# First fetches of a routed expert stage taken from the token table itself, with the work around them reordered

## The chip, the cores and the metric

One core of one Trainium2 chip runs the whole kernel. The metric is the device time in microseconds. TensorE is PE in the profile (PEld is its weight load), VectorE is DVE, ScalarE is ACT, GpSimd is POOL, SyncE is SP (SPq and POOLq are the queues that issue DMAs).

## The reference

The kernel computes two transformer blocks of two layers each on 512 tokens of width 1024. In the first block each layer has a mixer (gated delta rule, then sparse attention), a layer norm, and a hierarchical mixture of experts. Only the mixture matters here:

```python
grp_p = softmax(xt @ w_grp + b_grp);  grp_prob, grp_idx = top_k(grp_p, 1)
e_logits = (xt @ w_rt + b_rt) of the chosen group          # 4 groups of 4 experts
top_p, top_i = top_k(softmax(e_logits), 2)                 # two experts per token
gate = grp_prob * top_p / sum(top_p)
for each of 16 experts:                                    # hidden width 256
    hdn = silu(xt @ wg) * (xt @ wu)
    acc += gate[:, expert] * (hdn @ wd)
```

Everything is float32.

## The kernel before, in words

**The stage.** `stage_experts` (L1815) runs once per layer. Every (token, expert) pair, 1024 in all, gets a slot; slots are grouped in blocks of 128 rows that share an expert. There are at least 16 blocks and at most 24 (`MAX_BLOCKS`); in the profiled execution both layers have 16. A block is: fetch its 128 token rows from memory (`h_rows`) with an indirect DMA, turn them on TensorE, multiply with the expert's gate and up weights, apply silu and the product, multiply with the down weights, and store 128 x 1024 results (`moe_rows`).

**Exact products from halves.** The gate and up product runs in the type fp32r. Weights `f` and inputs are split into a high part `h` (a copy, on ACT, `hi` L1789) and a low part `l` (the difference, `lo` L1793, 128x2048 elements), and three products hh, hl, lh are added. The gate and up weights of a block come as two units of 1 MiB (`load_in`, u = 0 and 1), the down weights as one of 1 MiB (`load_down`). There are two sets of buffers, b = 0 and 1, used by even and odd blocks. The down product takes `f` as plain f32.

**Routing.** Before the first block `Route` finds the slots. On VectorE: `slots` (L1652 to L1706) computes the two experts of each token and its slots; `rows` (L1709 to L1727) writes two sets of one-hot matrices, `named` (block of the slot, times the token's number, L1718 to L1723) and `in_row` (row inside the block, L1725; before the change it lies in the buffer `rt_y`). TensorE multiplies them, eight products of 128x128 by 128x24 in f32 (L1648), which gives the table row by block of token numbers. `tables` (L1738 to L1750) writes the experts of the blocks and the number of loop turns to `rt.table`, with instructions on one partition; SyncE, TensorE, ScalarE and GpSimd read it by register once `tabled` is counted. `tokens` (L1729 to L1736) reads the product, and writes the token numbers to `route.tok` as integers (L1736), which counts `indexed`.

**What GpSimd does.** It waits for `h_kept` (the token rows are in memory) and `indexed`. Its helper `fetch(i, b)` copies column i of `route.tok` into a tile `mine[b]` (L2024), waits for `picked`, adds two constants into the tile `passed` (L2026), and issues the indirect DMA with `mine[b]` as indices (L2027), which counts `x_loaded[b]`. It does so for blocks 0 and 1 at once, for later blocks when the rows of the block before have been turned. It also makes the low part of unit 1 for all blocks from the second on.

**What VectorE does.** Its order is: `slots`, `rows`, `tables`, `tokens`, the low parts of both units of block 0, then the low part of the turned rows, then per block: the low part of unit 0 of the next block, the product for `hid` (L2071), the low part of the next rows (L2062).

**What SyncE issues,** in program order: the constants `marks`, unit 0 of block 0 (L1781), the store of the token rows (L1868, 2 MiB), unit 1 of block 0, the down weights of block 0 (L1785), the loads for the stage after (L1872: in the first layer two of 512 KB and two of 4 KB, in the second only one of 4 KB). Then it waits for the first fetch (`x_loaded[0]`), and issues units 0 and 1 and the down weights of block 1. Later weights go out when their buffer is free: `turn_over` waits for `lo_ready` of each unit.

**The order of a block on TensorE:** gate and up products (24 products L1951, unit 0 then unit 1), turning of the next block's rows (L1930), down product of the block before (L1942), turning of `hid` (L1964). ScalarE's order in `body` is: `hidden` of the block before, `hi` of the next block's two units, silu (L2006), high part of the next rows (L1989), then `take`, the copy of the block before's result into `rt_y` (L1996), which waits until the store before it has landed.

```python
for b in range(2):
    fetch(BlockCount(b), b)                 # GpSimd, L2035
fetch_next(BlockCount(1), 1)
```

## Time and profile before

| | us |
|---|---|
| median of 3 runs | 2588.68 |
| the runs | 2580.58, 2588.68, 2588.92 |
| profiled execution, its own time | 2579.54 |
| its span | 2577.7 |
| PE busy in the span | 2332.3 (90%) |
| mean granted clock of PE | 0.948 of full speed |
| expert stage, first layer | about 545 to 751 of the span |
| expert stage, second layer | about 1166 to 1370 of the span |

A granted clock of 0.50 in a window is TensorE at 1.2 GHz, 1.00 is 2.4 GHz. Times below are from the start of the span. In a row of the timeline, "[a <-b]" at the end says that the engine was idle for a us before it and that b ended the idle time. Rows that follow each other are merged (x2, x8), with their whole stretch as duration.

### The profile page before, as it was taken

The page shows a single profiled execution, that of the slowest core. Times are in us where ns is not written, and L with a number is a line of the kernel's source. Part 1 is how long each engine was busy: PE and PEld are TensorE (multiplying, and loading weights), DVE is VectorE, ACT ScalarE, POOL GpSimd, SP SyncE. Part 2 cuts the span into 40 slices and gives each one's busy share as a digit, 9 for nine tenths or more (in the row PEclk, how much of TensorE's full clock was granted, in tenths as well). Part 3 has the DMA queues.
Part 4 walks back from the last instruction along what each step waited for, and adds up shares of the span by engine and source line. Part 5 has one row for each costly group of instructions (what it writes and reads, how often), then busy time and mean ns, then how long its engine had stood idle before and what let it go on. Part 6 is the DMA issues. An engine that isn't in the chain of part 4 may idle for free. (4 is left out here: it accounts for less than half of the span.)

```text
span 2577.7 us, 32698 instructions
## 1 busy us (share of the span) xinstructions
PE 2332.3 (90%) x12304; PEld 1810.2 (70%) x12304; DVE 1147.9 (45%) x2271; ACT 1047.9 (41%) x1830; POOL 853.7 (33%) x375
## 2 busy tenths in 40 slices
PE   6999999759969989995994899999997999999998
PEld 5888888656747866674763667678886767668886
DVE  3654642354436358754434453562223354462122
ACT  4443442216643247723664334533223334533222
POOL 2433532415552310023562222334332312224442
PEclk9999999769989999996997999999999999999999
DMA  6113110239983331017995311224222511315212
GB/s 138 49 50 115 42 50 30 90 137 393 401 296 84 135 105 44 30 51 261 396 406 191 102 49 62 90 67 147 97 66 76 172 33 50 119 50 164 98 66 74
DMA packets 190956, 327.15 MB, mean 127 GB/s; under 512 B 52544, under 2 KB 103056, under 8 KB 178528
## 3 DMA queue, kind: packets, MB, share of 16 engines
q1 hardware_dynamic: 183904, 300.08, 34.2%
q0 software_dynamic: 6912, 25.17, 2.6%
q8 instruction: 92, 1.51, 0.2%
q14 instruction: 48, 0.39, 0.0%
HBM read 293.62 MB, written 31.60 MB: 126 GB/s over the span
## 5 line engine op out<-in xcount | busy, mean ns | idle before, releaser
L159 POOL TENSOR_TENSOR branch_weights_wl<-branch_weights_wf,branch_weights_wh 128x2048 fp32r<-128x2048 f32 (+1 forms) x66 | 301.8, 4574 | 770.7 <-ACT branch_weights_wh L153 770.7
L153 ACT ACTIVATE branch_weights_wh<-branch_weights_wf 128x2048 fp32r<-128x2048 f32 (+1 forms) x66 | 124.6, 1889 | 200.2 <-PE merge_acc L207 92.9
L544 POOL TENSOR_TENSOR in_weights_wl<-in_weights_wf,in_weights_wh 128x1024 fp32r<-128x1024 f32 x32 | 79.5, 2486 | 237.1 <-ACT in_weights_wh L540 219.3
L207 PE MATMUL bmid_acc<-xh,branch_weights_wh 128*128 128x512 f32 x320 | 148.7, 465 | 9.1 <-PEq L72 9.1
L207 PE MATMUL merge_acc<-xh,branch_weights_wh 128*128 128x512 f32 x384 | 152.3, 397 | 3.4 <-PEq L72 3.4
L159 POOL TENSOR_TENSOR nsa_weights_wl<-nsa_weights_wf,nsa_weights_wh 128x2048 fp32r<-128x2048 f32 x13 | 59.5, 4585 | 282.2 <-ACT nsa_weights_wh L153 282.2
L207 PE MATMUL merge_acc<-xl,branch_weights_wh 128*128 128x512 f32 x384 | 152.1, 396 | 0.0
L207 PE MATMUL merge_acc<-xh,branch_weights_wl 128*128 128x512 f32 x384 | 152.0, 396 | 0.0
L207 PE MATMUL bmid_acc<-xh,branch_weights_wl 128*128 128x512 f32 x320 | 127.4, 398 | 0.0
L207 PE MATMUL bmid_acc<-xl,branch_weights_wh 128*128 128x512 f32 x320 | 127.3, 398 | 0.0
L1942 PE MATMUL exp_ps_y<-rt_wf,exp_ht 128*128 128x512 f32 x256 | 115.4, 594 | 2.9 <-ACT exp_ht L1984 1.9
L3274 ACT ACTIVATE bmid_pt<-bmid_x 128x256 f32<-128x256 f32 (+3 forms) x128 | 55.8, 436 | 141.6 <-PE bmid_x L3241 141.6
L568 PE MATMUL gmain_acc<-xh,in_weights_wh 128*128 128x512 f32 x256 | 110.6, 432 | 0.0
L1793 POOL TENSOR_TENSOR rt_wl<-rt_wf,rt_wh 128x2048 fp32r<-128x2048 f32 x16 | 76.9, 4804 | 79.8 <-ACT rt_wh L1789 79.8
L568 PE MATMUL gmain_acc<-xl,in_weights_wh 128*128 128x512 f32 x256 | 102.0, 398 | 0.0
L568 PE MATMUL gmain_acc<-xh,in_weights_wl 128*128 128x512 f32 x256 | 101.8, 398 | 0.0
L3611 ACT ACTIVATE merge_gate<-merge_acc,merge_gb 128x512 f32<-128x512 f32 x48 | 33.1, 689 | 148.8 <-DVE merge_merged L3639 75.2
L3637 DVE TENSOR_TENSOR merge_gate<-merge_gate,merge_b 128x512 f32<-128x512 f32 x32 | 22.0, 687 | 159.9 <-PE merge_b L3563 159.7
L207 PEld LDWEIGHTS merge_acc<-xh,branch_weights_wh 128*128 128x128 f32 x384 | 72.3, 188 | 21.3 <-issue 4.2
L1951 PE MATMUL exp_ps_gu<-rt_wh,xl 128*128 128x512 f32 x256 | 86.6, 410 | 0.4 <-DVE xl L2062 0.4
L207 PEld LDWEIGHTS merge_acc<-xh,branch_weights_wl 128*128 128x128 f32 x384 | 72.3, 188 | 17.3
L207 PEld LDWEIGHTS merge_acc<-xl,branch_weights_wh 128*128 128x128 f32 x384 | 72.4, 189 | 17.2
(659 smaller groups left out, 6209.0 us busy)
## 6 DMA issues: line engine op xcount, KB each, us to landing
branch_weights_wf<-w_in SPq DMA_DIRECT2D x56, 1024.0 KB, 5.1
rt_wf<-moe_w_out SPq DMA_DIRECT2D x32, 1024.0 KB, 10.2
rt_wf<-moe_w_in SPq DMA_DIRECT2D x32, 1024.0 KB, 9.2
in_weights_wf<-gdn_w_in SPq DMA_DIRECT2D x64, 256.0 KB, 3.4
nsa_weights_wf<-moe_w_in SPq DMA_DIRECT2D x16, 1024.0 KB, 9.9
moe_rows<-rt_y SPq DMA_DIRECT2D x64, 256.0 KB, 8.9
branch_weights_wf<-moe_w_in SPq DMA_DIRECT2D x16, 1024.0 KB, 9.8
merge_bwf<-w_branch SPq DMA_DIRECT2D x12, 1024.0 KB, 5.0
```

Of the source, the lines that this page charges most:

```text
L153: act.activation(self.h[u][:, :, 0:self.cols(b)], self.s.f[u][:, :, 0:self.cols(b)], ACT.Copy).then_inc(self.s.hi_ready, 1)
L159: pool.tensor_tensor(self.l[u][:, :, 0:self.cols(b)], self.s.f[u][:, :, 0:self.cols(b)], self.h[u][:, :, 0:self.cols(b)].bitcast(F32), ALU ...
L207: mm = pe.matmul(self.acc[:, s, 0:cols], lhs[:, P * s:P * s + P], rhs, start=(u == 0 and k == 0 and n == 0), stop=(u == 1 and k == HALF - ...
L544: pool.tensor_tensor(self.l[n % 3][:], self.f[n % 3][:], self.h[n % 3][:].bitcast(F32), ALU.subtract).then_inc(self.lo_ready, 1)
L568: mm = pe.matmul(self.acc[:, tile % 3, :], w[n % 3][:, k, P * s:P * s + P], x[:, HALF * u + k, :], start=(u == 0 and k == 0 and m == 0), s ...
L1793: eng.tensor_tensor(self.l[b][u][:], self.f[b][u][:], self.h[b][u][:].bitcast(F32), ALU.subtract).then_inc(self.lo_ready[u], 1)
L1942: mm = pe.matmul(ps_y[:, c, :], ht[:, k, :], w[:, k, c, :], start=(k == 0), stop=(k == 1))
L1951: mm = pe.matmul(ps_gu[:, 0, :].rearrange("p (c n) -> p c n", c=2), x[:, HALF * u + k, :], ws.by_matrix(w[b][u])[:, :, k, :], start=(u == ...
L3274: act.activation(self.pt[:, e, 0:width], self.ps_t[:, 0:width], ACT.Copy).then_inc(self.copied, 1)
L3611: act.activation(gate[:, f % 2, :], ws.acc[:, f, :], ACT.Sigmoid, bias=gb[:, n, 4 * j + f:4 * j + f + 1]).then_inc(ws.evicted, 1)
L3637: dve.tensor_tensor(gate[:, f % 2, :], gate[:, f % 2, :], ps_b[:, f, :], ALU.mult).then_inc(b_out, 1)
```

## The change

GpSimd's first two fetches use columns 0 and 1 of `route.tok` as indices directly (`fetch_first`): no copy to `mine`, no wait for `picked`, no addition into `passed`. The count that later fetches wait for on `picked` falls by two to match. VectorE's order becomes `slots`, `rows`, low part of unit 0 of block 0, `tokens`, `tables`, low part of unit 1. The one-hot matrices that TensorE multiplies are written as fp32r: `in_row` gets a tile of its own, and `named` times the token number goes to a new tile `named_r`. SyncE issues both gate and up units of block 1 before it waits for the first fetch; after the wait it issues the down weights of blocks 0 and 1, and then the loads for the stage after. All of it is in both layers.

```diff
--- before.py
+++ after.py
@@ -1621,8 +1621,9 @@
             ("step", "g_diff", "second", "exps"))
         self.onehot, self.counted, self.tabled = st.sem("r_onehot"), st.sem("r_counted"), st.sem("r_tabled")
         self.rowed, self.placed, self.indexed = st.sem("r_rowed"), st.sem("r_placed"), st.sem("r_indexed")
-        self.marks, self.in_row = marks, rt.y[:].rearrange("p (n r) -> p n r", r=P)
+        self.marks, self.in_row = marks, st.sb("in_row", [P, 2 * TT, P], F32R)
         self.reached, self.named = st.sb("reached", [P, 2 * TT, MAX_BLOCKS - 1]), st.sb("named", [P, 2 * TT, MAX_BLOCKS])
+        self.named_r = st.sb("named_r", [P, 2 * TT, MAX_BLOCKS], F32R)
         self.zero = st.sb("zero", [P, 1], I32)
         self.block, self.row = st.sb("block", [P, 2 * TT]), st.sb("row", [P, 2 * TT])
         self.spare, self.tok = st.sb("spare", [P, MAX_BLOCKS]), st.sb("tok", [P, MAX_BLOCKS], I32)
@@ -1645,7 +1646,7 @@
         for n in range(2 * TT):
             if n % TT == 0:
                 pe.wait_ge(self.rowed, n // TT + 1)
-            mm = pe.matmul(self.ps[:, 0, P:P + MAX_BLOCKS], self.in_row[:, n, :], self.named[:, n, :],
+            mm = pe.matmul(self.ps[:, 0, P:P + MAX_BLOCKS], self.in_row[:, n, :], self.named_r[:, n, :],
                            start=(n == 0), stop=(n == 2 * TT - 1))
         mm.then_inc(self.placed, 1)
 
@@ -1720,7 +1721,7 @@
         name = marks[:, P + n:P + n + TT]
         for k in range(2):
             named = self.named[:, TT * k:TT * k + TT, :]
-            link(dve.tensor_tensor(named, named, name.unsqueeze(2).to_broadcast([P, TT, MAX_BLOCKS]), ALU.mult))
+            link(dve.tensor_tensor(self.named_r[:, TT * k:TT * k + TT, :], named, name.unsqueeze(2).to_broadcast([P, TT, MAX_BLOCKS]), ALU.mult))
         for k in range(2):
             dve.tensor_tensor(self.in_row[:, TT * k:TT * k + TT, :],
                               self.row[:, TT * k:TT * k + TT].unsqueeze(2).to_broadcast([P, TT, P]),
@@ -1867,13 +1868,13 @@
                 ws.load_in(sp, 0, 0, 0)
                 sp.dma_start(g.h_rows.rearrange("(t p) d -> p t d", p=P), g.h[:]).then_inc(h_kept, 16)
                 ws.load_in(sp, 0, 1, 0)
-                ws.load_down(sp, 0, 0)
+                for u in range(2):
+                    ws.load_in(sp, 1, u, 1)
+                sp.wait_ge(x_loaded[0], 16)
+                for b in range(2):
+                    ws.load_down(sp, b, b)
                 for x, src in rt.loads:
                     sp.dma_start(x, src).then_inc(ln_in, 16)
-                sp.wait_ge(x_loaded[0], 16)
-                for u in range(2):
-                    ws.load_in(sp, 1, u, 1)
-                ws.load_down(sp, 1, 1)
 
                 def store(i):
                     for c in range(2):
@@ -2020,9 +2021,13 @@
 
             @block.gpsimd
             def _(pool):
+                def fetch_first(b):
+                    pool.indirect_dma_start(xr[b][:], None, g.h_rows[:, :],
+                                            bass.IndirectOffsetOnAxis(route.tok[:, b:b + 1], 0)).then_inc(x_loaded[b], 16)
+
                 def fetch(i, b):
                     pool.tensor_tensor(mine[b][:], route.tok[:, bass.ds(i(), 1)], route.zero[:], ALU.add).then_inc(picked, 1)
-                    pool.wait_ge(picked, i(1, 1))
+                    pool.wait_ge(picked, i(1, -1))
                     pool.tensor_tensor(passed[:], marks[:, 0:1], marks[:, 1:2], ALU.add)
                     pool.indirect_dma_start(xr[b][:], None, g.h_rows[:, :],
                                             bass.IndirectOffsetOnAxis(mine[b][:], 0)).then_inc(x_loaded[b], 16)
@@ -2033,7 +2038,7 @@
                 pool.wait_ge(h_kept, 16)
                 pool.wait_ge(route.indexed, 1)
                 for b in range(2):
-                    fetch(BlockCount(b), b)
+                    fetch_first(b)
                 fetch_next(BlockCount(1), 1)
                 pool.wait_ge(ws.lo_ready[1], 1)
                 ws.lo(pool, 1, 1, BlockCount(2))
@@ -2053,8 +2058,10 @@
                 dve.wait_ge(ld, 16)
                 route.slots(dve)
                 route.rows(dve)
+                ws.lo(dve, 0, 0, BlockCount(1))
+                route.tokens(dve)
                 route.tables(dve)
-                route.tokens(dve)
+                ws.lo(dve, 0, 1, BlockCount(1))
 
                 def x_lo(i):
                     for v in range(2):
@@ -2071,8 +2078,6 @@
                     dve.tensor_tensor(hid[:], act_g[:], ps_gu[:, 0, HID:512], ALU.mult).then_inc(hid_done, 1)
                     if not last:
                         x_lo(i.plus(1))
-                for u in range(2):
-                    ws.lo(dve, 0, u, BlockCount(1))
                 x_lo(BlockCount(0))
 
                 def scale():
```

## Rows read from the trace of the kernel before

**Rows 1.** Windows view, steady stretch: us, each engine's busy us (records), PEclk, DMA share, GB/s

```profile
640.00:660.00 20.00, 20.00 (x85) 13.99 (x84) 8.01 (x8) 13.10 (x16) 12.12 (x9) 1.00 1.02 416
```

**Rows 2.** Timeline, first layer, routing to first gate-up product: start, us, engine, line

```profile
559.72 1.29 DVE L1725 TENSOR_TENSOR rt_y<-exp_row,exp_marks 128x512 f32<-128x512 f32 x2
...
560.46 3.61 PE L1648 MATMUL exp_ps_t<-exp_named,rt_y 128*128 128x24 f32 x16 [5.86 <-DVE rt_y L1725]
...
564.11 0.24 DVE L1734 TENSOR_SCALAR exp_spare<-exp_ps_t,exp_marks 128x24 f32<-128x24 f32 x1 [1.45 <-PE exp_ps_t L1648]
...
564.69 4.49 DVE L1793 TENSOR_TENSOR nsa_weights_wl<-nsa_weights_wf,nsa_weights_wh 128x2048 fp32r<-128x2048 f32 x2
...
564.93 2.09 POOL L2024 TENSOR_TENSOR exp_mine<-exp_tok,exp_zero 128x1 int32<-128x1 int32 x1 [61.19 <-DVE exp_tok L1736]
...
569.40 1.12 POOL L2027 DMA_INDIRECT exp_xr<-h_rows,exp_mine  x1 [0.17 <-issue]
...
573.87 0.80 SPq L1781 DMA_DIRECT2D rt_wf<-moe_w_in  x2
...
576.52 0.77 PE L1951 MATMUL exp_ps_gu<-nsa_weights_wh,xl 128*128 128x512 f32 x1 [0.65 <-DVE xl L2062]
```

**Rows 3.** Windows view, the stretch while the fetch is being prepared

```profile
565.00:570.00 5.00, 0.00 (x0) 0.00 (x0) 4.18 (x2) 0.00 (x0) 4.75 (x3) 0.50 0.00 0
```

**Rows 4.** Timeline, first layer, between the first and the second block

```profile
584.79 1.03 PE L1930 MATMUL exp_ps_x<-ident,exp_xr 128*128 128x128 f32 x8
...
584.91 1.91 ACT L1789 ACTIVATE rt_wh<-rt_wf 128x2048 fp32r<-128x2048 f32 x1 [1.67 <-DMA rt_wf<-moe_w_in]
...
588.14 0.38 ACT L2006 ACTIVATE exp_act_g<-exp_ps_gu 128x256 f32<-128x256 f32 x1
...
589.88 0.76 PE L1951 MATMUL exp_ps_gu<-rt_wh,xl 128*128 128x512 f32 x1 [0.22 <-DVE xl L2062]
```

**Rows 5.** Timeline, first layer, second block's end and third block

```profile
596.76 1.03 PE L1930 MATMUL exp_ps_x<-ident,exp_xr 128*128 128x128 f32 x8
...
596.96 0.39 ACT L2006 ACTIVATE exp_act_g<-exp_ps_gu 128x256 f32<-128x256 f32 x1 [2.47 <-PE exp_ps_gu L1951]
...
601.21 0.48 PE L1951 MATMUL exp_ps_gu<-nsa_weights_wh,xl 128*128 128x512 f32 x1
...
606.80 1.03 PE L1930 MATMUL exp_ps_x<-ident,exp_xr 128*128 128x128 f32 x8
```

**Rows 6.** Timeline, second layer, end of first and of second block's gate-up products

```profile
1203.94 1.03 PE L1930 MATMUL exp_ps_x<-ident,exp_xr 128*128 128x128 f32 x8
...
1210.28 0.77 PE L1951 MATMUL exp_ps_gu<-rt_wh,xl 128*128 128x512 f32 x1 [0.16 <-DVE xl L2062]
...
1217.54 1.03 PE L1930 MATMUL exp_ps_x<-ident,exp_xr 128*128 128x128 f32 x8
```

**Rows 7.** Timeline, a fetch beside a low part on VectorE

```profile
592.05 2.35 DVE L1793 TENSOR_TENSOR nsa_weights_wl<-nsa_weights_wf,nsa_weights_wh 128x2048 fp32r<-128x2048 f32 x1 [1.72 <-ACT nsa_weights_wh L1789]
...
592.07 0.96 POOL L2027 DMA_INDIRECT exp_xr<-h_rows,exp_mine  x1
```

**Rows 8.** Timeline, the queue of SyncE, first layer

```profile
548.58 1.83 SPq L1872 DMA_DIRECT2D nsa_weights_ln_vectors<-ln_ffn_g  x1
...
552.89 1.21 SPq L1872 DMA_DIRECT2D nsa_weights_norm_shift<-by_feature  x1
...
574.72 0.59 SPq L1785 DMA_DIRECT2D rt_wf<-moe_w_out  x1
...
576.92 1.13 SPq L1781 DMA_DIRECT2D nsa_weights_wf<-moe_w_in  x2
```

**Rows 9.** Timeline, first layer, the last two of 16 blocks

```profile
714.00 1.31 ACT L1996 ACTIVATE rt_y<-exp_ps_y 128x512 f32<-128x512 f32 x2 [4.57 <-DMA moe_rows<-rt_y]
...
729.22 4.87 POOL L1793 TENSOR_TENSOR rt_wl<-rt_wf,rt_wh 128x2048 fp32r<-128x2048 f32 x1 [5.09 <-ACT rt_wh L1789]
...
732.32 0.48 PE L1951 MATMUL exp_ps_gu<-rt_wh,xl 128*128 128x512 f32 x1
```

## The prediction

> **What bounds the kernel now.** I first read the windows view over the first layer's expert stage. In its steady part TensorE is busy for all of every 20 us at full clock, and the DMA engines are busy all the time too, moving 416 GB/s [rows 1]. So two resources are at their limit together, and the question is which sets the pace. A block needs 4 MiB: 3 MiB of weights, half a MiB of fetched rows, half a MiB of stores. The third block's first gate-up product starts at 601.21 and the sixteenth's at 732.32 [rows 5, 9]: 13 blocks in 131.1 us, 10.09 each. TensorE's own work accounts for it: gate and up take 601.21 to 606.80, 5.59, and from there to the next block's first product 4.45 pass (596.76 to 601.21) [rows 5]; 5.59 + 4.45 = 10.04. From the third block on, TensorE sets the end, and what brings the third block forward brings the stage's end forward. The other demand, 4.19 MB in 10.09 us, is 416 GB/s: the transfers just keep up.
>
> Ahead of the third block the timeline shows TensorE waiting. The one-hot matrices are done at 561.01 (559.72 + 1.29), the table product starts at 560.46 and lasts 3.61, VectorE reads it from 564.11. GpSimd starts at 564.93, needs 2.09 for the copy of one column and as much for the addition, and issues the fetch at 569.40. SyncE sees the rows land at 573.87, and TensorE starts gate and up at 576.52 [rows 2]. While the fetch is prepared no byte moves [rows 3]. After the first block TensorE is late again: the second block's weights go out at 573.87, behind the fetch [rows 2]; ScalarE waits for their second unit, which it copies at 584.91, and only then does the first block's silu, at 588.14, though TensorE was through with gate and up at 584.79. The second block starts at 589.88 [rows 4].
>
> **The fetch, part by part.** Removed on GpSimd: the copy, the wait and the addition. From VectorE's start on the product (564.11) to GpSimd's first instruction 0.82 pass, and from there to the issue 4.47 [rows 2]. The 4.47 go, up to some 0.15 that a wait takes to end. The two are that long because VectorE's two low parts run just then (4.49 from 564.69, 2.24 each) [rows 2]. The Trainium skill (SBUF — State Buffer, Who interferes with whom) says that a VectorE instruction with two inputs in SBUF shuts out a GpSimd instruction that reads SBUF, for its whole length; by that rule the copy, which starts and ends with a low part, waited for the lock, and the trace agrees; the change removes it either way.
>
> Added ahead of `tokens` on VectorE: one low part, 2.24. It starts when the one-hot matrices are done, 561.05, and ends at 563.3. Beside it TensorE does the product. In f32 this is 8 products in 16 records over 3.61 [rows 2]; as fp32r I take one record each, half the time, 1.8: it ends by about 562.4, under the low part. (If the type saved nothing, it would end at 564.07 as now, and 0.8 of the gain below would go.) `tokens` starts at 563.3, the fetch goes out at 563.3 + 0.82 = 564.12 instead of 569.40: **5.28 earlier**. I keep the landing at 573.87 - 569.40 = 4.47 after the issue and the first gate-up product 2.65 after that (576.52 - 573.87) [rows 2]: 571.24.
>
> Moved behind `tokens`: `tables`, under 2 us of one-partition instructions, and the low part of unit 1, from about 565.8 to 568.1. Both lie under the flight of the fetch; the low part of the turned rows is not wanted before 570.4. SyncE needs the table only after the fetch has landed. Their cost is nothing as long as the fetch takes over 4 us; without that cover it would be 4. The new tile takes no time, and the writes as fp32r have the same elements; between nothing and 0.1 each I take nothing.
>
> **The weights.** Both units of block 1 now fill the idle stretch. In the first layer 6 MiB go ahead of the fetch before and after (the down weights and 1 MiB for the next stage change places with these two), so the queue is empty by 565 as in rows 3. In the second layer the next stage's loads are small: 1 MiB more goes ahead, 1.05 MB / 416 GB/s = 2.5 us [rows 1], about done when the fetch goes out. If the fetch and its neighbour share with it, the fetch lands up to 1.3 later (half a MiB); I take 0.
>
> With unit 1 in SBUF, ScalarE copies both units right after the turned rows, done by 575.1, and is free when gate and up end. The first block's gate-up took 584.79 - 576.52 = 8.27, part of it at the low clock (0.50 in the window before, rows 3). All at full clock it is 5.59, all at half 11.2: a gain of 2.7 or a loss of 2.9; I keep 8.27, since the same idle stretch stands before it. It ends at 579.51. In the undisturbed second block silu starts 0.20 after that point [rows 5], and the next block starts 1.74 after silu [rows 4]: 1.94 instead of 589.88 - 584.79 = 5.09. **3.15 gained**; should the table load ahead of silu not hide, 1.3 less. In the second layer the same gap is 1210.28 - 1203.94 = 6.34 [rows 6]: **4.40 gained**.
>
> The second block's gate-up took 596.76 - 589.88 = 6.88 [rows 4, 5], in the second layer 1217.54 - 1210.28 = 7.26 [rows 6]: after the idle wait the clock was low again. With TensorE idle for under 1 us at a time I take the full-clock 5.59: **1.29** and **1.67**; bounds are nothing and these.
>
> **What is late next.** The third block's weights. SyncE now has two down loads and, in the first layer, the next stage's loads (from 548.58 to 552.89 + 1.21 = 554.10, 5.5 of issuing [rows 8]) between the fetch and `turn_over`. Landing is seen at 568.6; 1.3 for the downs, 5.5, and the 1.6 that passed between 575.31 and 576.92 [rows 8] give 577.0: the very time of now. The queue holds 3 MiB and a fetch by then, gone by 577.3. The two units land near 582 and 584.5 (2.5 of transfer each, and an estimated 2 until it is seen); ScalarE is ready at 581.9. Its copies end at 586.4, GpSimd's low part (4.87 [rows 9]) at 591.3, and TensorE wants it at 591.6 + 2.8 = 594.4. That leaves 3.1 of margin. In the second layer the 5.5 are nearly absent. The down weights of block 0, moved past the fetch, land by 573 and are wanted at 588.
>
> **Sum.** First layer 5.28 + 3.15 + 1.29 = 9.72; second 5.28 + 4.40 + 1.67 = 11.35; together 21.1. One us off for margins that close late: at the last block GpSimd ends at 734.09 what TensorE wants at 732.32 + 2.8 = 735.1 [rows 9], 1.0 to spare in the first layer. **20 us.** The profiled execution took 2579.54 (span 2577.7 and 1.84 around it), which would give 2559.5. The median of the runs shown is 2588.68, 9.1 above; I set the gain against that: **2568.7**.
>
> **Rivals.** (1) The transfers set the pace, chance 0.2. ScalarE waits 4.57 for a store's landing late in the first layer [rows 9], so transfers have little left. Then the end moves only as the stream does: it restarts 5.28 earlier, and carries 1 MiB (2.5) less in the second layer: 13.1, plus the 1.0 that is spare. 14 us, 2574.7. Against it: TensorE's busy 20 of 20 [rows 1].
> (2) The fetch does not come earlier, chance 0.08: VectorE's low part of unit 1 or the weight loads hold it. For it, the copy of 2.09 in rows 2. Against it: a later fetch was issued in 0.96 beside a low part begun 0.02 before [rows 7]. The weights' part stays: 3.15 + 1.29 + 4.40 + 1.67 = 10.5, 2578.2. Were only the issue held, for one low part of 2.24 in each layer, 20 - 4.5 gives 15.5, 2573.2; rows 7 speak against it, `tables` stand between, and it has 0.03 of this 0.08. The Trainium skill's rule of SBUF — State Buffer, cited above, would do this if the fetch's reading of its indices counts as a read.
> (3) Little is left, chance 0.06: the early start is used up in both layers because the third block's weights are late by more than their 3.1 margin and the steady part starts no earlier than 4 us before now. Gain under 7.8.
> (4) Slower, chance 0.03. Place: ScalarE's wait for the store before it may write `rt_y` again; low parts of the next block queue behind. If TensorE starts earlier but stores land later, this loop can pass TensorE's 10.09. It costs 26 blocks times the excess; from 21.1 / 26 = 0.8 us per block on, all is lost, and at 1.1 the time is 7.5 above now, 2596.2. The 4.57 wait shows the loop is real [rows 9]; nothing in the change lengthens a store.
>
> **Chances and range.** What a measurement here can tell from no change is about 0.3%, 7.8 us. Forecast 0.63 and rivals (1) and (2) lie beyond it except for a part: faster 0.87, same 0.10, slower 0.03. The range takes in (1) and (2) at the upper end. At the lower end stands the full gain with the first blocks at the fast clock (21.1 + 5) from the median, 2562.6, or 20 from the lower level of the runs, 2560.6, with some room: 2556 to 2581.
>
> **What would show it.** The indirect DMA at about 564 and 1184.5, with no L2024 ahead of it; first gate-up product near 571.2; silu of the first block within 0.5 of gate-up's end; the second block's gate-up in 5.6; third block at 591.5 in the first layer; then 10.09 per block. Wrong: the third block early but the sixteenth not (rival 1), a fetch that lands more than 5.5 after its issue (2), ScalarE waiting for the third block's weights (3), a period above 10.4 (4).

## The result and the profile after

The changed kernel takes 2570.86 us (median of four runs, 2566.31 to 2572.63) against 2588.48 before (four runs, 2580.58 to 2588.92): a ratio of 0.9936, 95% interval 0.9913 to 0.9960. 2568.7 was forecast. The gain is 17.6 where 20 were expected, clear of no change and clear of the 0.3% that can be told here. Run again later, beside other kernels, it took 2568.10 against 2584.98, ratio 0.9938 (0.9921 to 0.9954).

The profiled execution took 2566.31, its span is 2564.5. The first rows are the timeline of the changed kernel, first layer, from the one-hot matrices to the first gate-up product, and answer to [rows 2]:

```profile
563.03 1.29 DVE L1726 TENSOR_TENSOR exp_in_row<-exp_row,exp_marks 128x512 fp32r<-128x512 f32 x2
563.78 1.88 PE L1649 MATMUL exp_ps_t<-exp_named_r,exp_in_row 128*128 128x24 f32 x8 [5.86 <-DVE exp_in_row L1726]
564.24 2.28 DVE L1794 TENSOR_TENSOR nsa_weights_wl<-nsa_weights_wf,nsa_weights_wh 128x2048 fp32r<-128x2048 f32 x1
...
566.45 0.23 DVE L1735 TENSOR_SCALAR exp_spare<-exp_ps_t,exp_marks 128x24 f32<-128x24 f32 x1
...
568.01 1.11 POOL L2025 DMA_INDIRECT exp_xr<-h_rows,exp_tok  x1 [62.21 <-DVE exp_tok L1737]
...
568.75 2.27 DVE L1794 TENSOR_TENSOR nsa_weights_wl<-nsa_weights_wf,nsa_weights_wh 128x2048 fp32r<-128x2048 f32 x1
569.42 2.42 POOL L2025 DMA_INDIRECT exp_xr<-h_rows,exp_tok  x1 [0.30 <-issue]
572.41 0.80 SPq L1786 DMA_DIRECT2D rt_wf<-moe_w_out  x2
...
575.05 0.76 PE L1952 MATMUL exp_ps_gu<-nsa_weights_wh,xl 128*128 128x512 f32 x1 [0.65 <-DVE xl L2069]
```

Absolute times do not compare, since this execution's stage began 3.31 later (548.61 against 545.30) with nothing changed ahead of it; in the twelve executions below it began anywhere from 544.26 to 548.07. So I count from the stage's first DMA issue in each layer, and write 19.40 for 568.01 - 548.61. The table product takes 8 records and 1.88 instead of 16 and 3.61, and hides under the low part. The fetch goes out at 19.40, before at 24.10. The *second* fetch's issue takes 2.42 where the first takes 1.11: a low part on VectorE began 0.67 before it.

Next, the timeline between first and second block, which answers to [rows 4] and [rows 5]. Silu now follows the end of gate and up (582.32) at once, the second block starts 2.10 after that end instead of 5.09, and its gate-up takes 5.67 instead of 6.88:

```profile
582.32 1.03 PE L1931 MATMUL exp_ps_x<-ident,exp_xr 128*128 128x128 f32 x8
582.51 0.39 ACT L2007 ACTIVATE exp_act_g<-exp_ps_gu 128x256 f32<-128x256 f32 x1 [2.58 <-PE exp_ps_gu L1952]
...
584.42 0.47 PE L1952 MATMUL exp_ps_gu<-rt_wh,xl 128*128 128x512 f32 x1 [0.57 <-DVE xl L2069]
...
590.09 1.04 PE L1931 MATMUL exp_ps_x<-ident,exp_xr 128*128 128x128 f32 x8
```

Then, still in the first layer, something that the forecast did not have. The timeline of the third block:

```profile
587.59 1.91 ACT L1790 ACTIVATE nsa_weights_wh<-nsa_weights_wf 128x2048 fp32r<-128x2048 f32 x1 [3.28 <-DMA nsa_weights_wf<-moe_w_in]
...
590.72 1.91 ACT L1790 ACTIVATE nsa_weights_wh<-nsa_weights_wf 128x2048 fp32r<-128x2048 f32 x1 [1.21 <-DMA nsa_weights_wf<-moe_w_in]
...
592.71 4.60 POOL L1794 TENSOR_TENSOR nsa_weights_wl<-nsa_weights_wf,nsa_weights_wh 128x2048 fp32r<-128x2048 f32 x1 [7.41 <-ACT nsa_weights_wh L1790]
...
594.82 2.51 DVE L1757 SCALAR_TENSOR_TENSOR exp_sg<-exp_e,exp_sg 128x4 f32<-128x4 f32 x1
...
597.77 6.98 DVE L2087 TENSOR_SCALAR h<-h 128x1024 f32<-128x1024 f32 x4
...
599.66 4.53 POOL L1794 TENSOR_TENSOR rt_wl<-rt_wf,rt_wh 128x2048 fp32r<-128x2048 f32 x1 [0.38 <-ACT rt_wh L1790]
...
604.67 2.28 DVE L1794 TENSOR_TENSOR rt_wl<-rt_wf,rt_wh 128x2048 fp32r<-128x2048 f32 x1
...
606.87 0.41 DVE L2078 TENSOR_TENSOR exp_hid<-exp_act_g,exp_ps_gu 128x256 f32<-128x256 f32 x1
...
607.34 0.44 PE L1965 MATMUL exp_ps_t<-ident,exp_hid 128*128 128x128 f32 x2 [2.56 <-DVE exp_hid L2078]
```

ScalarE waits for the third block's weights. GpSimd's low part of them runs to 597.31, and VectorE's instruction on 4 elements per partition, begun inside it, takes 2.51 and ends with it. The scaling of the rows (L2087, in the helper `scale`, once per stage) then takes 6.98. GpSimd's next low part begins inside it and ends at 604.19, and the scaling ends soon after. Behind it VectorE still has its own low part of the next block to make (604.67), and only then comes the `hid` product; TensorE waits 2.56. Which of VectorE's instructions is the one held is a matter of tenths: when this same kernel ran again (e11), the scaling got through and the low part behind it was held, with the same loss. Before, the same scaling fell between two low parts on GpSimd and took 2.50. This is the timeline of the kernel before:

```profile
594.57 4.57 POOL L1793 TENSOR_TENSOR nsa_weights_wl<-nsa_weights_wf,nsa_weights_wh 128x2048 fp32r<-128x2048 f32 x1 [1.54 <-ACT nsa_weights_wh L1789]
...
600.03 2.50 DVE L2082 TENSOR_SCALAR h<-h 128x1024 f32<-128x1024 f32 x4
...
606.34 4.83 POOL L1793 TENSOR_TENSOR rt_wl<-rt_wf,rt_wh 128x2048 fp32r<-128x2048 f32 x1 [5.50 <-ACT rt_wh L1789]
```

All kernels in one table. The positions are starts in the profiled execution, counted from the stage's first DMA issue, first / second layer. "hid 2" and "hid 16" are where TensorE turns (transposes) `hid` of the second and the sixteenth block (the loss just shown lies between hid 2 and hid 3, 12.9 where it should be 10.0; some expectations below call these the third and fourth block); the ratio is to the kernel before, run alongside.

| kernel | median us | ratio (95%) | fetch issued | hid 2 | hid 16 |
|---|---|---|---|---|---|
| before | 2588.48 | | 24.10 / 23.41 | 55.77 / 55.44 | 197.43 / 195.81 |
| changed | 2570.86 | 0.9936 (0.9913-0.9960) | 19.40 / 18.56 | 45.79 / 45.36 | 189.52 / 185.73 |
| e1 copies back | 2565.44 | 0.9927 (0.9904-0.9950) | 19.05 / 18.70 | 45.21 / 45.94 | 191.08 / 188.15 |
| e2 weights back | 2568.88 | 0.9944 (0.9930-0.9959) | 18.98 / 18.50 | 47.89 / 46.05 | 188.27 / 186.42 |
| e3 VectorE order back | 2576.83 | 0.9973 (0.9960-0.9986) | 18.43 / 17.98 | 47.72 / 45.88 | 195.24 / 186.25 |
| e4 f32 product | 2567.09, one run | | 20.11 / 19.61 | 47.44 / 45.64 | 187.81 / 185.98 |
| e5 scaling early | 2564.46 | 0.9913 (0.9892-0.9935) | 18.97 / 18.50 | 47.04 / 45.41 | 188.54 / 189.05 |
| e6 norm loads late | 2565.19 | 0.9921 (0.9898-0.9943) | 19.13 / 18.54 | 45.89 / 45.58 | 186.26 / 187.74 |
| e7 both (e5, e6) | 2567.18 | 0.9922 (0.9897-0.9946) | 19.40 / 18.50 | 47.04 / 45.05 | 187.41 / 185.41 |
| e8 VectorE order alone | 2571.12 | 0.9946 (0.9928-0.9963) | 20.37 / 19.62 | 48.36 / 48.26 | 188.70 / 193.60 |
| e9 two result buffers | 2566.59 | 0.9930 (0.9916-0.9945) | 19.34 / 18.56 | 45.73 / 45.43 | 188.96 / 185.72 |
| e10 e9 and e6 | 2561.84 | 0.9906 (0.9888-0.9924) | 19.01 / 18.59 | 45.32 / 45.44 | 185.61 / 185.73 |
| e11 changed again | 2568.10 | 0.9938 (0.9921-0.9954) | 18.97 / 19.64 | 45.76 / 45.92 | 189.33 / 186.29 |
| e12 e6 again | 2563.82 | 0.9920 (0.9904-0.9935) | 19.36 / 18.63 | 45.96 / 45.45 | 186.33 / 188.69 |

The gain of the two profiled executions splits like this. Up to hid 16 the first layer gained 197.43 - 189.52 = 7.91, the second 195.81 - 185.73 = 10.08, together 18.0. The rest of the kernel, unchanged, was 4.8 later (3.31 ahead of the first stage, 1.03 between the stages, 0.45 behind the second), which leaves the 13.2 that the spans differ by. The medians, over several runs, show 17.6, close to the stages' own 18.0. What lies outside the two stretches up to hid 16 took anywhere from 2184.4 to 2195.0 in the fourteen profiled executions, though no edit aims at it. That is more than most of the kernels below differ by, so a single execution's time says little, and the readings below go by positions inside the stage.

### The profile page after: what moved, and what is told of

Same layout as the page of the kernel before. It is cut to its first block and busy times, and to the rows that moved or that the text cites. A ratio compares the mean times of both kernels' runs of the same rounds, so it can differ in the third digit from the quotient of the medians.

```text
span 2564.5 us, 32648 instructions
## 1 busy us (share of the span) xinstructions
PE 2327.3 (91%) x12288; PEld 1804.1 (70%) x12288; DVE 1156.2 (45%) x2271; ACT 1046.7 (41%) x1830; POOL 850.1 (33%) x367
## 5 line engine op out<-in xcount | busy, mean ns | idle before, releaser
L727 ACT ACTIVATE gmain_x<-gmain_chunk 128x512 f32<-128x512 f32 x48 | 28.7, 597 | 137.1 <-PE gmain_chunk L658 137.1
```

The lines of the kernel that those rows point to most:

```text
L727: act.activation(self.x[i], self.B[i], ACT.Copy).then_inc(self.x_out[i], 1)
```

## The experiments

### e1: the copies back

```diff
-                    pool.wait_ge(picked, i(1, -1))
+                    pool.wait_ge(picked, i(1, 1))
...
                 for b in range(2):
-                    fetch_first(b)
+                    fetch(BlockCount(b), b)
```

> The changed kernel, but its first two fetches go through the copies again (copy, wait, addition, indirect DMA); all orders stay changed. Two readings of the two 2.1 us instructions before the change. Theory A (they were held by VectorE's low parts, and the new order of VectorE alone frees them): each takes 0.2, the first fetch is issued 18.9 to 19.6 after the stage's first DMA issue, where the changed kernel has 19.4 and 18.56 in its two layers, and the time is that of the changed kernel within 2 us, some 17 below before. Theory B (GpSimd's first instructions in a stage are slow by themselves, 2.1 each): the fetch goes out about 3.6 later in each layer and the time is about 7 us above the changed kernel.

Timeline of this kernel, first layer, GpSimd (the low part of unit 1 on VectorE begins at 564.95):

```profile
563.54 0.19 POOL L2029 TENSOR_TENSOR exp_mine<-exp_tok,exp_zero 128x1 int32<-128x1 int32 x1 [61.05 <-DVE exp_tok L1737]
563.81 0.19 POOL L2031 TENSOR_TENSOR exp_passed<-exp_marks 128x1 f32<-128x1 f32 x1
564.36 1.12 POOL L2032 DMA_INDIRECT exp_xr<-h_rows,exp_mine  x1 [0.36 <-issue]
565.51 1.76 POOL L2029 TENSOR_TENSOR exp_mine<-exp_tok,exp_zero 128x1 int32<-128x1 int32 x1
```

Theory A holds: 0.19 each instead of 2.09. The fourth row is the counterproof in the same trace: the copy for the second block, under a low part, takes 1.76. The fetch goes out at 19.05 and 18.70, no later than without the copies (19.40 and 18.56), since a direct fetch starts only 0.9 after the token numbers are written (566.93 + 0.18 to 568.01 in the changed kernel). Under the new order of VectorE the direct fetch, the part after which the change is named, is worth nothing that can be measured; the median is even lower than the changed kernel's, within the scatter. What it does under the old order shows in e3.

### e2: the weights back

```diff
-                for u in range(2):
-                    ws.load_in(sp, 1, u, 1)
-                sp.wait_ge(x_loaded[0], 16)
-                for b in range(2):
-                    ws.load_down(sp, b, b)
+                ws.load_down(sp, 0, 0)
                 for x, src in rt.loads:
                     sp.dma_start(x, src).then_inc(ln_in, 16)
+                sp.wait_ge(x_loaded[0], 16)
+                for u in range(2):
+                    ws.load_in(sp, 1, u, 1)
+                ws.load_down(sp, 1, 1)
```

> The changed kernel, but SyncE issues in the order of before: block 0's down weights and the next stage's loads first, both units of block 1 only after the first fetch has landed. Theory A (the pace is TensorE's, and the third block's start carries over to the end): the first fetch stays early, silu of the first block waits for ScalarE's copies again, the third block starts 4.4 later in the first layer and 5.5 to 6 later in the second than in the changed kernel, and the time is about 10 above it, 7.5 below before. Theory B (transfers set the pace): the same bytes go before the fetch in the first layer, so nothing is lost there, and 2.5 in the second.

Theory A had the direction and not the size. hid 2 comes 2.10 later in the first and 0.69 later in the second layer, not 4.4 and 5.5. ScalarE's copy of unit 1 starts 9.60 and 8.12 after SyncE's issue of the two units, where it started 11.04 and 11.15 after it before the change. The same loads land up to 3 sooner than before the change, because the DMA engines carry them faster (windows view under e3). At the end of the first layer this kernel is even ahead of the changed one (188.27 against 189.52): with its later second block the scaling misses GpSimd's low part. But the edit does two things. It also puts the next stage's loads back ahead of the fetch, out of the way of the third block's weights, which is what e6 does by other means. Beside e6 (186.26), which keeps the early weights, e2 is 2.0 late. So the early weights give 0.7 in the second layer and some 2 in the first, and in the changed kernel's first layer the place of the next stage's loads takes that back.

### e3: VectorE's order back

```diff
-                ws.lo(dve, 0, 0, BlockCount(1))
-                route.tokens(dve)
                 route.tables(dve)
-                ws.lo(dve, 0, 1, BlockCount(1))
+                route.tokens(dve)
+                for u in range(2):
+                    ws.lo(dve, 0, u, BlockCount(1))
```

> The changed kernel, but VectorE does tables, tokens, then both low parts, as before. GpSimd's first fetch is then ready to issue about 0.9 after tokens, inside the first low part. Theory A (a low part on VectorE that has begun holds an indirect DMA's issue on GpSimd until it ends): the issue record is 2 us or longer or begins after a low part's end, and the rows land 1.3 to 3.6 later than in the changed kernel; 2.5 to 7 us on the time. Theory B (the issue is not held, as one record of 0.96 beside a low part seemed to show): the fetch goes out 0.3 earlier than in the changed kernel and the time is the same or 1 us better.

Timeline, first layer, both engines:

```profile
561.70 4.49 DVE L1794 TENSOR_TENSOR nsa_weights_wl<-nsa_weights_wf,nsa_weights_wh 128x2048 fp32r<-128x2048 f32 x2
562.69 2.28 POOL L2025 DMA_INDIRECT exp_xr<-h_rows,exp_tok  x1 [59.78 <-DVE exp_tok L1737]
565.28 1.73 POOL L2025 DMA_INDIRECT exp_xr<-h_rows,exp_tok  x1 [0.30 <-issue]
```

The issue is held, 2.28 in both layers instead of 1.0 to 1.1. But it also starts 1.0 and 0.6 earlier, and the rows are seen at 24.05 and 23.71, only 0.25 and 0.85 later than in the changed kernel: theory A's mechanism, well under its price. Against the kernel before, the rows still land 4.5 and 4.1 sooner, with VectorE's order as it was: dropping the copies and the shorter product bring that. So the new order and the direct fetch stand in for each other, and either alone brings most of the early fetch (for the order alone see e8).

The time is 6 to 9 above the changed kernel's all the same. The profiled execution, the fastest of the ten, shows 5.7 of it behind the fetch, in the first layer: from hid 1 on the blocks follow each other by 12.6, 14.2 and 13.1 before they settle at 10.04. That is the loss of the third block's weights, larger: ScalarE copies its units at 41.59 and 45.03, in the changed kernel at 38.98 and 42.11.

SyncE issues them 1.6 later than in the changed kernel (29.94, there 28.36), as the next stage's loads took it 3.4 instead of 2.1, and the transfers are slow just after the fetch. Here is the windows view some 3 to 6 us after the first rows are seen, first layer, in the kernel before, in e3 and in e8 (the last number is GB/s, the one ahead of it the busy share of the DMA engines):

```profile
577.00:579.00 2.00, 2.00 (x6) 1.54 (x5) 0.23 (x1) 0.00 (x0) 0.51 (x1) 0.50 1.04 299
572.00:574.00 2.00, 2.00 (x6) 1.60 (x5) 1.23 (x1) 2.00 (x2) 0.00 (x0) 0.50 0.96 332
575.00:577.00 2.00, 2.00 (x6) 1.52 (x6) 0.00 (x0) 0.00 (x0) 0.22 (x1) 0.50 0.97 406
```

In the stretch from 4 to 6 us after the rows are seen, both layers of the kernel before and of e3 move 279 to 340 GB/s, and the other 24 layers profiled 377 to 442. The first two are the ones with the old order of VectorE. (In e3's second layer, where the next stage's loads are small, the slow stretch costs next to nothing by hid 16: 186.25 against 185.73.) With one profiled execution of each this goes with the order; how an order of VectorE could slow DMA transfers no run here shows.

### e4: the product in f32

```diff
-        self.marks, self.in_row = marks, st.sb("in_row", [P, 2 * TT, P], F32R)
+        self.marks, self.in_row = marks, st.sb("in_row", [P, 2 * TT, P])
...
-        self.named_r = st.sb("named_r", [P, 2 * TT, MAX_BLOCKS], F32R)
+        self.named_r = st.sb("named_r", [P, 2 * TT, MAX_BLOCKS])
```

> The changed kernel, but the table product in f32 again (16 records for 8 products). If it takes 3.6 as before it ends about 0.8 to 0.9 after VectorE's low part, and tokens and the fetch come 0.9 later in each layer than in the changed kernel (issue about 19.4 to 20.3 after the stage's first DMA issue): 1.8 in all. If the low part still covered it, nothing.

The fetch is 0.71 and 1.05 later, as expected. The stage is not: hid 16 comes at 187.81 in the first layer, 1.7 *before* the changed kernel. Its timeline shows why:

```profile
596.62 2.62 DVE L2087 TENSOR_SCALAR h<-h 128x1024 f32<-128x1024 f32 x4
599.16 2.28 DVE L1794 TENSOR_TENSOR rt_wl<-rt_wf,rt_wh 128x2048 fp32r<-128x2048 f32 x1
599.94 5.91 POOL L1794 TENSOR_TENSOR rt_wl<-rt_wf,rt_wh 128x2048 fp32r<-128x2048 f32 x1 [1.80 <-ACT rt_wh L1790]
```

Here GpSimd's low part comes 0.7 after the scaling has ended and 0.8 after VectorE's own low part has begun, and it is GpSimd that waits (5.91 instead of 4.53), with time to spare. In the changed kernel it comes inside the scaling, before VectorE's low part, and VectorE waits. Which of the two low parts begins first decides on 3 us.

### e5: the scaling early

```diff
+                scale()
                 x_lo(BlockCount(0))
...
-                _, last = pairs(dve, body, scale)
+                _, last = pairs(dve, body)
```

> The changed kernel, but VectorE scales the rows and computes the gate weights (the helper scale) while it waits for the first fetch, not after the second block. Theory A (in the first layer the scaling, held by GpSimd's low parts, makes the third block's hidden product late, 2.9 us): the fourth block's turning of hid follows the third's by 10.0 instead of 12.9 in the first layer, the sixteenth comes 186 to 187 after the stage's start instead of 189.5, the second layer stays at 185.7 within 0.7; time 2 to 3 below the changed kernel. Theory B (the late weights of the third block are what costs, the scaling is only in between): the gap stays near 12.9.

Neither as expected. The scaling takes 2.50 in the wait for the fetch, at no cost. But in this execution the third block's second unit landed still later (copied at 44.35, not 42.11), hid 2 came 12.6 after hid 1 instead of 11.0, and hid 3 another 11.2 later. The first layer ends at 188.54: 1.0 won, not 3. So the late weights cost by themselves, and the scaling adds to it; what the early scaling would give with weights on time is what e7 shows in its first layer, nothing beyond e6. The second layer fell into a stretch of slow blocks (below), and this execution was the slowest of its seven. By its ratio the kernel is not told from the changed one.

### e6 and e12: the next stage's loads behind the weights

```diff
-                for x, src in rt.loads:
-                    sp.dma_start(x, src).then_inc(ln_in, 16)
...
                     turn_over(BlockCount(i), i % 2)
+                    if i == 3:
+                        for x, src in rt.loads:
+                            sp.dma_start(x, src).then_inc(ln_in, 16)
```

> The changed kernel, but SyncE issues the next stage's loads (two of 512 KB in the first layer) after the gate and up units of the third and fourth block, not ahead of them. The third block's first unit is issued about 26.7 after the stage's start instead of 28.4, with 1 MiB less ahead of it, and ScalarE copies it at 35 to 37 instead of 39.0. Theory A: GpSimd's low parts then miss the scaling as in the second layer, the fourth block's hid follows the third's by 10.0, the sixteenth comes at 186 to 187 in the first layer, time 2 to 3 below the changed kernel. Theory B (transfers late by themselves, the 1 MiB costs wherever it goes): the loss of 2.9 moves to a later block and the time stays.

> The kernel with the late loads for the next stage again, beside the changed kernel in the same call. Theory A (the 1 MiB ahead of the third block's weights is what costs 2 to 3 in the first layer): median 2 to 3 below the changed kernel and 10.0 from the third to the fourth block. Theory B (noise of transfers): same median within 1.5 and a late fourth block in this one too.

Theory A, in both. ScalarE copies the third block's units at 35.68 and 38.10 (e6), GpSimd's low part begins at 40.09 instead of 44.10, hid 3 follows hid 2 by 10.0, and hid 16 comes at 186.26 and 186.33 in the first layer, against 189.52 and 189.33 for the changed kernel in its two profiles: **3.1 us**. Run side by side, the medians are 2563.82 and 2568.10. The two intervals overlap (0.9904 to 0.9935, 0.9921 to 0.9954), so the 4.3 of the medians rest on the traces more than on the times.

### e7: both

> Both of the two edits. If they take away the same loss, once, the time is that of either of them, 2 to 3 below the changed kernel, and about 20 below before; if the two are separate losses, 4 to 6 below the changed kernel.

The edits are those of e5 and e6 together. One loss, not two: no block after the second takes over 10.2 in either layer (first layer 187.41, with a first gate-up of 8.40 at the lower clock), and the median, 2567.18, is no better than e5's or e6's.

### e8: VectorE's order alone, on the kernel before

```diff
                 route.rows(dve)
-                route.tables(dve)
+                ws.lo(dve, 0, 0, BlockCount(1))
                 route.tokens(dve)
+                route.tables(dve)
+                ws.lo(dve, 0, 1, BlockCount(1))
...
-                for u in range(2):
-                    ws.lo(dve, 0, u, BlockCount(1))
                 x_lo(BlockCount(0))
```

> The kernel of before with one part of the change: VectorE's order (low part of unit 0, tokens, tables, low part of unit 1). Product in f32, the copies on GpSimd, SyncE's order as before. Theory A (this order is what frees the copies and the fetch): the two copies take 0.2 each, the first fetch goes out 20.0 to 20.5 after the stage's start instead of 24.10 and 23.41, and 13 to 16 us of the time go. Theory B (the direct fetch and the early weights carry the gain): at most 2 us go.

Theory A. The fetch goes out at 20.37 and 19.62, and hid 2 comes 7.4 and 7.2 before that of the kernel before, where the whole change has 10.0 and 10.1. In the first layer the 7.4 are 3.7 from the earlier fetch, 2.5 from ScalarE's copy of unit 1 coming sooner after it (13.0 after the issue, before 15.5: the transfers, as in e3), and 1.2 from the second gate-up. The median falls by 12.2, short of the 13 to 16 expected. The profiled execution has a stretch of blocks at 10.6 to 10.8 in the second layer, which costs it 5.0; whether the other six had one was not recorded. Here is that stretch in the windows view, in e8, and below in e2, which had none:

```profile
1240.00:1260.00 20.00, 20.00 (x85) 13.87 (x84) 7.69 (x8) 12.63 (x16) 10.96 (x9) 1.00 1.00 387
1280.00:1300.00 20.00, 19.16 (x81) 13.23 (x80) 6.16 (x8) 11.09 (x14) 11.67 (x8) 1.00 1.02 401
```

And e2:

```profile
1240.00:1260.00 20.00, 20.00 (x85) 13.95 (x84) 8.01 (x8) 13.17 (x18) 12.30 (x9) 1.00 1.02 421
1280.00:1300.00 20.00, 20.00 (x85) 13.94 (x84) 8.01 (x8) 13.16 (x17) 12.33 (x9) 1.00 1.02 420
```

The DMA engines are as busy in both but move 387 to 401 GB/s in one and 420 in the other. A block at 10.09 wants 416. This looks like rival 1, in some layers of some executions: the second layers of e1, e5, e6, e8 and e12 have such blocks and lose 1.8 to 5.0 by them, the other nine profiled executions have none.

### e9 and e10: two result buffers

```diff
-        y = rt.y
+        y = [rt.y, st.sb("y1", [P, D])]
+        unused = st.sb("unused", [P, 32])
...
+                for c in range(2):
+                    sp.dma_start(unused[:, 16 * c:16 * c + 16], a["c_marks"][:, 0:16]).then_inc(y_stored[c], 16)
                 sp.wait_ge(x_loaded[0], 16)
```

The results of even and odd blocks go to `y[0]` and `y[1]`. The two small loads raise the count of stores by one, so that the wait that was for the last store is for the one before it. e10 has the edit of e6 as well.

> The changed kernel with a second buffer for a block's result, so that ScalarE waits for the store before the last one and not for the last. Some layers in the runs so far have a stretch of blocks at 10.6 to 10.8 instead of 10.04 to 10.14, with the DMA engines busy all the time at 385 to 400 GB/s. Theory A (the wait of ScalarE for the store's landing turns slow transfers into late low parts; the transfers as such have room): no wait for stores is left, no block over 10.3 in either layer but for the fourth of the first layer, and the runs spread less, 3 to 5 below the changed kernel in the median. Theory B (transfers are the limit in such a stretch): blocks at 10.6 and more still come, median within 2 of the changed kernel.

> The second result buffer and the late loads for the next stage together. If both act: sixteenth block's hid at 186 to 187 in the first and 185 to 186 in the second layer, median 5 to 8 below the changed kernel. If only the late loads act, 2 to 3.

> The changed kernel itself, unaltered, in the same call as the others, so that versions can be compared at 0.2%. Its ratio to before should come out at 0.9936 within 0.0015 again, and the fourth block of the first layer should be 12 to 14 after the third where its weights land late, as in the first profile.

e11, the changed kernel again, repeats the first result: ratio 0.9938, hid 3 of the first layer 12.8 after hid 2. But the instruction that is held is another. The scaling takes 2.62 and is through, and VectorE's low part behind it takes 6.60, in the timeline of e11:

```profile
596.79 4.98 POOL L1794 TENSOR_TENSOR rt_wl<-rt_wf,rt_wh 128x2048 fp32r<-128x2048 f32 x1 [0.49 <-ACT rt_wh L1790]
...
597.32 6.60 DVE L1794 TENSOR_TENSOR rt_wl<-rt_wf,rt_wh 128x2048 fp32r<-128x2048 f32 x1
```

e9 is the same in this (6.61). So it is not the scaling as such: late weights set VectorE's whole chain back until GpSimd's second low part begins ahead of VectorE's.

e9's second layer ran without a slow stretch, so did e11's, and both with the same hid 16 within 0.6. The wait for stores nearly goes from the list of waits; its lines (total us, times, longest) read, in e12:

```profile
ACT rt_y L1998 <- DMA moe_rows<-rt_y: 79.6, 27, 4.8
```

In e10 ScalarE waits before the same instruction mostly for TensorE, and 8.9 in all for stores:

```profile
ACT exp_y L2001 <- PE exp_ps_y L1947: 32.5, 28, 2.2
ACT rt_y L2001 <- PE exp_ps_y L1947: 26.3, 24, 1.1
ACT exp_y L2001 <- DMA moe_rows<-rt_y: 4.5, 4, 1.1
ACT rt_y L2001 <- DMA moe_rows<-exp_y: 4.4, 4, 1.1
```

Whether the second buffer carries a layer over slow transfers could not be seen, so neither theory was tested: no profile with it caught any (e10 moved 417 to 422 GB/s where e12 moved 379 to 394). e9's median is 1.5 below e11's, within the scatter. e10 has the lowest median of the study: **2561.84**, four runs between 2559.04 and 2563.06, ratio 0.9906 (0.9888 to 0.9924), with hid 16 at 185.61 and 185.73. The changed kernel took 2568.10 beside it, 6.3 more, which is in the 5 to 8 expected if both edits act; but the intervals of the two still touch, and e12, with the late loads alone, took 2563.82, so the second buffer's share is not shown.

## Why the prediction was right, and where it was off

**What bounds the kernel** was right. In every profile TensorE returns to a period of 10.04 and 10.14 in turn, and what the third block gained is there at the end, unless something takes it on the way. The sum of the stages came out by cancelling, though: 20.1 gained up to hid 2, 3.4 lost at the third and fourth block of the first layer, and 1.3 gained at that layer's last block, which the forecast did not have. It found 1.0 to spare on GpSimd there. The kernel before lost 1.3 there to something else: the down weights, issued at 730.50, landed at 739.12, and the down product, 1.05 late, starts right behind. From the timeline of the kernel before:

```profile
739.22 3.67 PE L1942 MATMUL exp_ps_y<-rt_wf,exp_ht 128*128 128x512 f32 x8 [1.05 <-issue]
```

That the total lies within 2.2 of the forecast is in part luck.

**The first two blocks** were right in sum and less so in terms. To hid 2 the forecast had 9.72 and 11.35, the profiles show 9.98 and 10.08:

| term | forecast | first layer | second layer |
|---|---|---|---|
| fetch issued earlier | 5.28 | 4.70 | 4.85 |
| landing | 0 | 0.07 | 0.05 |
| first gate-up | 0 | 1.00 | -0.66 |
| gap to second block | 3.15 / 4.40 | 2.99 | 4.24 |
| second gate-up | 1.29 / 1.67 | 1.21 | 1.59 |

The fetch term was over by 0.5 because I took GpSimd to issue 0.82 after VectorE's start on `tokens`, the time it needed for a copy; it was 1.56 (566.45 to 568.01). The first gate-up scatters between 6.9 and 8.4 over all profiles, as the clock rises sooner or later in it: its granted clock was 0.65 and 0.77 in the two layers before, 0.75 and 0.70 after. Keeping it was a fair middle, and that its two errors nearly cancel is luck. That the second gate-up runs at the full clock once TensorE is not kept waiting held in both layers (5.67 at 1.00 in each, before 6.88 at 0.81 and 7.26 at 0.76).

**What I credited** was half wrong, and the sum hid it. I gave 4.47 to the removal of the copies and took the reordering for a way to hide the product. e1 and e8 show that the reordering alone does it, and e3 that the direct fetch (with the shorter product) does most of it too where the order stays. Each has its worth only where the other is missing. The Trainium skill (SBUF — State Buffer, Who interferes with whom) has the rule, and I had quoted it: a VectorE instruction with two inputs in SBUF holds up a GpSimd instruction that reads SBUF. I did not draw its consequence, that moving the low parts away makes the copies 0.19, so that behind the reordering their removal is worth 0.4 at most.

**The weights** were valued at 3.15 + 1.29 and 4.40 + 1.67, and are worth 2.1 and 0.7 up to hid 2 (e2), because without them the second block is not as late as it was: the two terms were read from a profile in which the fetch was late and the transfers behind it slow.

**What was late next** is the step that failed. The third block's weights were named, with a margin of 3.1. They were seen 2.3 and 2.9 later than forecast (38.98 and 42.11 from the start, against 36.7 and 39.2), and GpSimd's low part ended at 48.7, which is just when TensorE wanted it (45.96 + 2.8): no margin left. SyncE had not been slow, since the next stage's loads took it 2.1 and not 5.5 to issue; it was the transfer, 10.6 from issue to copy behind 3 MiB and two fetches. And `scale` was not looked at, as the change does not touch it. It was hidden before because it fell into a gap of GpSimd, and the change moved that gap. In my one us for margins that close late there was room for a third of the 2.9 + 0.5 that the third and fourth block lost.

**Rival 1** (transfers set the pace) fits single layers, five of the 28 profiled. **Rival 2**'s mechanism, a low part that holds the issue of a fetch, I argued away with [rows 7]: one issue of 0.96 that stood 0.02 *behind* a low part in the trace. e3 and the second fetch of the changed kernel (2.28, 2.42) show that the hold exists. In the changed kernel it meets a fetch that is not needed yet, so the price was right for another reason. **Rival 3** (late weights of the third block) came in the first layer by its own mark, ScalarE waiting 3.28 and 1.21 for them, but not in the second; it took 3.4 and not the whole gain. **Rival 4** did not come.

## What to carry to other kernels

An instruction that is long for its size may be held by another engine: before it is removed, see what runs beside it, and try moving that away. A change that brings work forward also shifts every once-per-stage step that fell into a gap, so list them with the gap each uses; here one scaling of 2.5 us turned into 7, or the instruction behind it into 6.6. Loads that nobody waits for belong behind those that somebody does: putting 1 MiB of them behind the units of two more blocks gave 3 us of a stage for nothing. When two parts of a change are priced one by one, ask what each is worth once the other is in: here either brought most of the early fetch.

## What the runs showed of the hardware

- VectorE and GpSimd hold each other up in both directions, and whoever has begun keeps going: a copy of one column takes 0.19 alone and 1.74 to 2.23 under a low part; an instruction of VectorE on 4 elements per partition takes 0.16 alone and 2.51 under GpSimd's low part; the scaling takes 2.50 and 6.98; VectorE's low part takes 2.28 and 6.60; GpSimd's low part takes 4.53 and 5.91 when VectorE was first.
- The hold takes in the issue of an indirect DMA: 2.28 to 2.84 beside a low part of VectorE that had begun 0.3 to 1.0 before, 1.73 and 1.84 beside one begun 1.4 and 1.3 before (e3), 1.42 beside the scaling, 0.95 to 1.13 otherwise. In the two cases where the low part had begun only some 0.03 before ([rows 7] and its like in the second layer) the issue was not held (0.96), and the low part took 2.35 and 2.36 instead of 2.28. The Trainium skill (SBUF — State Buffer, Who interferes with whom) infers that a two-input subtraction or addition spares descriptor generation. For a DMA that reads its indices from SBUF these records say otherwise. Whether the indices or the descriptors are what waits, no run here shows.
- A direct indirect DMA starts 0.8 to 0.9 after the token numbers it waits for are written; behind a short instruction of GpSimd's own it starts after 0.14 to 0.36.
- The same transfers, with all DMA engines busy, move 420 GB/s in one execution and 380 to 400 in another. What decides it stayed open. It costs such a layer 1.8 to 5.0; the rest of the kernel scatters by 10.6 besides.
- Just after the first fetch the same transfers moved 279 to 340 GB/s in the two kernels with VectorE's old order and 377 to 442 in the twelve others. The cause is not shown.
